# Down weight sums kept in HBM, activation sums on VectorE, and a buffer of its own for the token halves' difference, in the second feed-forward part of a Hymba layer

## The chip, the cores and the metric

The kernel is one program on one core of a Trainium2 chip. Its engines run side by side and meet at semaphores: TensorE (PE in the profile), VectorE (DVE), ScalarE (ACT), GpSimd (POOL) and SyncE (SP), which issues the transfers. The metric is the time of one execution in microseconds (us), the median of the runs.

## The reference

One layer of a Hymba decoder on 1024 tokens of 1024 features in float32: a half-step feed-forward part, a mixer (dilated attention and a Mamba-2 scan), and a second feed-forward part. The change lies in the second one:

```python
def swiglu(x, w_gate, w_up, w_down):
    return (jax.nn.silu(x @ w_gate) * (x @ w_up)) @ w_down
...
h = swiglu(rmsnorm(x, ffn2_pre_norm[i]), ffn2_w_gate[i], ffn2_w_up[i], ffn2_w_down[i])
x = x + MACARON_WEIGHT * rmsnorm(h, ffn2_post_norm[i])
```

D_FF is 2816, which makes 22 tiles of 128 hidden features, or 11 groups of two.

## The kernel before

Every float32 operand of a matmul is split in two parts that TensorE takes: hi is a rounded copy (a cast on ACT), lo is the operand less hi (a subtraction on DVE). A product is then three matmuls, hi by hi, lo by hi and hi by lo.

The second feed-forward part (f2) runs in four stages.

1. **The turn** (about 1610 to 1642 us). The first two hidden tiles are computed plainly, in rounds 0 to 3 of PE (gate_up matmuls, lines L560 to L562), while the layer's x is still being finished. Beside it DVE and ACT form the token operands that the later stage needs: s1, s2, s4 and `x_difference`, the difference of the first and the second half of the tokens (`difference`, L948 to L950, into the buffer d3, which shares its place with what rounds 0 to 2 read), times a gain, split in norm_hi and norm_lo. A planner (`turn_plan`) with a cost, the steps it depends on and a rank for each step writes the order of every engine. Lines L991 to L1013 prepare the first tile's gate and up operands.
2. **The rounds** (1642 to 2025 us). The other 20 tiles, in ten pairs i = 1 to 10 with s = 0 and 1. A tile is a block product in seven products instead of eight, with sums of gate and up weights (t_raw) and of tokens (s): product 1 to 7 of 12 matmuls each. `ffn_sp` loads each next tile, first its gate block, then two up blocks (L387, L390: g_next, v_next), each as soon as its buffer is read out, and stores the activations of the tile before to `act_scratch` in HBM (L425).
3. **Down** (2025 to 2265 us). The down projection is again seven products, m = 0 to 6, of 11 k-groups of 12 matmuls (L1517 to L1519, `down_three`). The tables DOWN_W and DOWN_B say which blocks of weights and activations product m takes: five of the seven weight operands and five of the seven activation operands are sums or differences of two blocks. For a weight sum SP loads two blocks of 256 KB (L1442) and POOL adds them (L1476, `down_w_sum`, 55 times); activation sums are on DVE for m = 1, 2, 3 and on POOL for m = 5, 6 (L1482, `down_b_sum`). Each k-group has its own slot, which product m+1 may fill when product m has used it (`down_slot`). hi parts: L1490 and L1504 on ACT. lo parts: L1508 and L1513 on DVE. `end_plan` orders all of it. `down_start_sp` starts it.
4. **The last norm.** Squares of the finished sums are added up on DVE (`square_sums`, L1758), added over features by matmuls with ones (columns, L1665), and the reciprocal root is spread over the rows by another (L1683), first for the first half of tokens, within the down products.

## Time and profile before

| what | value |
|---|---|
| median of 3 runs | 2276.1 us (2273.67 to 2276.16) |
| profiled execution, own time | 2276.56 us |
| its span in the trace | 2274.8 us |
| PE busy | 2209.6 us, 97% |
| DVE busy | 1741.1 us, 77% |
| ACT busy | 965.1 us, 42% |
| POOL busy | 350.4 us, 15% |

The span is what the trace covers; 1.8 us of the execution's time lie around it. A row of a timeline gives start, duration, engine, line and operation, tiles read and written, and in brackets how long the engine was idle ahead of it and what ended that. Times of matmuls are pipelined: 0.39 us each, but one starts every 0.227 us.

### The profile page before, as it was taken

Reading aid. Unit: us, or ns where it says so; the run is one execution under the profiler, and the core shown is the slowest. Engines: PE = TensorE matmul, PEld = TensorE weight load, DVE = VectorE, ACT = ScalarE, POOL = GpSimd, SP = SyncE. Lnnn points to the kernel's source line nnn. Section 1 sums busy time; section 2 is a strip of 40 time slices with the busy share of each in tenths; the row PEclk is TensorE's granted clock in tenths of the full one; section 3 lists DMA queues with packets and bytes.
Section 4 is the critical chain, followed back from the end, with each engine's and each line's share of the span. In section 5 each row is a group of like instructions: output and inputs, shape, how many; then the busy total and the mean of one; then the engine's idle time right before and its main releaser. Section 6 shows DMA issues by size and latency. Waiting matters only on the chain.

```text
span 2274.8 us, 29629 instructions
## 1 busy us (share of the span) xinstructions
PE 2209.6 (97%) x10304; PEld 1809.2 (80%) x10304; DVE 1741.1 (77%) x2550; ACT 965.1 (42%) x1725; POOL 350.4 (15%) x290
## 2 busy tenths in 40 slices
PE   9999999999999999999999999999899999989989
PEld 7888888888877877778788777788788888868867
DVE  8877777777759777786666676878877777789997
ACT  6322222222334576787531674224422323335443
POOL 0000000000000344444100225100000000033572
PEclk9999999999999999999999999999999999999999
DMA  4111111111323001001121234132122222285734
GB/s 161 54 53 43 54 55 55 55 40 47 117 98 125 20 10 38 29 18 57 59 82 47 75 119 174 60 100 105 53 87 83 83 83 83 83 312 201 231 116 148
DMA packets 78179, 199.83 MB, mean 88 GB/s; under 512 B 8448, under 2 KB 10496, under 8 KB 76288
## 3 DMA queue, kind: packets, MB, share of 16 engines
q1 hardware_dynamic: 78080, 198.56, 26.0%
q8 instruction: 57, 0.93, 0.2%
q14 instruction: 42, 0.34, 0.0%
HBM read 165.69 MB, written 32.83 MB: 87 GB/s over the span
## 4 chain that ended last, share of the span: by engine, by line
PE 84%; DVE 7%; ACT 3%; issue 3%; POOL 2%; DMA 1%; SPq 0%; DVEq 0%; ACTq 0%; POOLq 0%
PE psum L473 11%; PE psum L474 11%; PE psum L475 11%; PE psum L641 4%; PE psum L643 4%; PE psum L642 4%; PE psum L2437 3%; PE psum L2439 3%; PE psum L2438 3%; PE psum L1517 3%; PE psum L1519 3%; PE psum L1518 3%; PE psum L2583 2%; PE psum L2980 1%; PE psum L2594 1%
## 5 line engine op out<-in xcount | busy, mean ns | idle before, releaser
L1476 POOL TENSOR_TENSOR down_w_raw<-down_w_raw,down_w_two 128x512 f32<-128x512 f32 x55 | 88.0, 1611 | 665.0 <-DMA down_w_two<-in_d 664.9
L770 ACT CAST t_hi<-t_raw 128x512 fp32r<-128x512 f32 x152 | 93.6, 621 | 204.4 <-DVE t_raw L991 151.3
L1190 DVE TENSOR_TENSOR acc<-psum,acc 128x512 f32<-128x512 f32 x144 | 98.9, 691 | 80.5 <-PE psum L643 79.1
L792 ACT ACTIVATE sum<-sum 128x512 f32<-128x512 f32 x76 | 48.1, 633 | 231.7 <-DVE sum L1130 139.7
L1517 PE MATMUL psum<-down_b_hi,down_w_hi 128*128 128x512 f32 x308 | 123.0, 400 | 8.9 <-DVE down_w_lo L1508 8.9
L2437 PE MATMUL psum<-norm_hi,tile_hi 128*128 128x512 f32 x320 | 129.1, 403 | 1.9 <-DVE z_scaled L2845 1.9
L2754 DVE TENSOR_TENSOR probs_t_lo<-psum,probs_t_hi 128x512 fp32r<-128x512 f32 x144 | 97.1, 685 | 39.8 <-ACT probs_t_hi L2671 38.9
L473 PE MATMUL psum<-norm_hi,plain_hi 128*128 128x512 f32 x304 | 119.2, 392 | 7.5 <-DVE up_lo L1013 7.5
L2439 PE MATMUL psum<-norm_hi,tile_lo 128*128 128x512 f32 x320 | 125.0, 391 | 0.0
L2438 PE MATMUL psum<-norm_lo,tile_hi 128*128 128x512 f32 x320 | 124.8, 390 | 0.0
L766 ACT CAST plain_hi<-up_raw 128x512 fp32r<-128x512 f32 x76 | 47.1, 619 | 180.7 <-DMA up_raw<-in_gu 177.9
L2532 POOL TENSOR_TENSOR q_k_next<-first_q_k,cos 128x512 f32<-128x512 f32 x6 | 8.0, 1353 | 748.9 <-DVE first_q_k L2499 748.9
L1518 PE MATMUL psum<-down_b_lo,down_w_hi 128*128 128x512 f32 x308 | 121.8, 396 | 0.0
L1519 PE MATMUL psum<-down_b_hi,down_w_lo 128*128 128x512 f32 x308 | 121.8, 395 | 0.0
L475 PE MATMUL psum<-norm_hi,up_lo 128*128 128x512 f32 x304 | 119.0, 391 | 0.0
L474 PE MATMUL psum<-norm_lo,plain_hi 128*128 128x512 f32 x304 | 119.0, 391 | 0.0
L473 PE MATMUL psum<-norm_hi,t_hi 128*128 128x512 f32 x304 | 118.3, 389 | 0.0
L475 PE MATMUL psum<-norm_hi,t_lo 128*128 128x512 f32 x304 | 118.3, 389 | 0.0
L473 PE MATMUL psum<-s_hi,t_hi 128*128 128x512 f32 x304 | 118.3, 389 | 0.0
L474 PE MATMUL psum<-s_lo,t_hi 128*128 128x512 f32 x304 | 118.3, 389 | 0.0
L475 PE MATMUL psum<-s_hi,t_lo 128*128 128x512 f32 x304 | 118.3, 389 | 0.0
L474 PE MATMUL psum<-norm_lo,t_hi 128*128 128x512 f32 x304 | 118.3, 389 | 0.0
(456 smaller groups left out, 6477.9 us busy)
## 6 DMA issues: line engine op xcount, KB each, us to landing
down_w_raw<-in_d SPq DMA_DIRECT2D x77, 256.0 KB, 2.9
gate_raw<-in_gu SPq DMA_DIRECT2D x38, 512.0 KB, 4.3
up_raw<-in_gu SPq DMA_DIRECT2D x76, 256.0 KB, 3.9
raw_tile<-in_w_att SPq DMA_DIRECT2D x28, 512.0 KB, 3.6
down_w_two<-in_d SPq DMA_DIRECT2D x55, 256.0 KB, 4.4
act_scratch<-act_stage SPq DMA_DIRECT2D x21, 512.0 KB, 5.2
tile_lo_raw<-in_d SPq DMA_DIRECT2D x20, 512.0 KB, 4.2
x_scratch<-acc SPq DMA_DIRECT2D x32, 256.0 KB, 2.0
```

The source lines that it names most:

```text
L473: pe.matmul(o, w_hi[:, k, :], a_hi(k), start=(k == 0 and not more), stop=False, skip_group_check=more)
L474: pe.matmul(o, w_hi[:, k, :], a_lo(k), start=False, stop=False, skip_group_check=more)
L475: mm = pe.matmul(o, w_lo[:, k, :], a_hi(k), start=False, stop=(k == KH - 1), skip_group_check=more)
L770: act.copy(to, of).then_inc(sem(p + "_t_hi"), 1)
L1190: v.tensor_tensor(x, banks(4 + d % 4), x, ALU.add).then_inc(sem(p + "_acc"), 1)
L1517: pe.matmul(o, dw_hi[k][:, d, :], db_hi[k][:], start=(k == 0), stop=False)
L1518: pe.matmul(o, dw_hi[k][:, d, :], db_lo[k][:], start=False, stop=False)
L1519: return pe.matmul(o, dw_lo[k][:, d, :], db_hi[k][:], start=False, stop=(k == FG - 1))
L2437: pe.matmul(banks(bank), wh[:, w % 2, k, :], nh[:, k, x], start=(k == 0), stop=False)
L2438: pe.matmul(banks(bank), wh[:, w % 2, k, :], nl[:, k, x], start=False, stop=False)
L2439: mm = pe.matmul(banks(bank), wl[:, w % 2, k, :], nh[:, k, x], start=False, stop=(k == KT - 1))
L2754: v.tensor_tensor(ptl[:, n % 2].rearrange("p a d -> p (a d)"), banks(4 + n % 2), pth[:, n % 2].rearrange("p a d -> p (a d)").bitcast(F32), ...
```

## The change

1. *Weight sums.* POOL forms the five sums or differences of the down weights once for each k-group, during the rounds. For each of the 11 groups SP loads the two row blocks whole (two transfers of 512 KB, `w_sum_in`) at the end of a tile's loads, POOL does four operations (`w_sum_pool`: one of 128x1024 and three of 128x512), and SP stores the five sums (1.31 MB, `w_sum_out`) to a new HBM tensor `down_w_sums` in the next tile. Of the tiles n = 0 to 18 the loads stand in n = 0, 1, 3, 4, 6, 7, 9, 10, 12, 13 and 15. In the down stage every operand of weights is then one load of 256 KB, 77 in place of 132, and POOL has nothing to do there. SP's loop over the rounds is written out.
2. *Activation sums.* All 55 are on DVE.
3. *Difference.* `x_difference_turn` has its own buffer in f2. The step no longer waits for round 2, and the first t_raw sums no longer wait for the low parts of the difference. The ranks of t_hi, t_sum and t_lo in the turn are changed.

```diff
-DOWN_W = (((1, 0), (1, 1), ALU.add), ((0, 0), (1, 1), ALU.add), ((1, 1),), ((0, 1), (1, 1), ALU.subtract),
-          ((0, 0), (0, 1), ALU.add), ((0, 0),), ((1, 0), (0, 0), ALU.subtract))
+DOWN_W = {2: (1, 1), 5: (0, 0)}
+W_SUM = {4: 0, 0: 1, 1: 2, 3: 3, 6: 4}
-POOL_B = (5, 6)
...
+        d3_turn = at("x_difference_turn", 164, [P, KH, HALF])
+        wsum = nc.dram_tensor("down_w_sums", (FG, P, 5, 4, P), F32).ap()
...
             if p == "f2":
...
-                with sp.Fori(2, LAST_PAIR) as i:
-                    g_next(i, 0)
-                    v_next(i, 0, 0)
-                    store(i - 1, 1)
-                    v_next(i, 0, 1)
...
+                for n in range(2 * LAST_PAIR - 1):
+                    i, s = 1 + n // 2, n % 2
+                    g_next(i, s)
+                    v_next(i, s, 0)
+                    if n:
+                        store(1 + (n - 1) // 2, (n - 1) % 2)
...
+                    v_next(i, s, 1)
...
+                    for k in range(FG):
+                        if 3 * k // 2 == n:
+                            w_sum_in(sp, k)
+                        if 3 * k // 2 + 1 == n:
+                            w_sum_out(sp, k)
...
             def difference():
-                wait(v, p + "_gu_mm", 2 if t == "t0" else 3)
-                v.tensor_tensor(d3[:], acc[:, 0:KH, half(0)], acc[:, 0:KH, half(1)], ALU.subtract).then_inc(sem(p + "_s_dve"), 1)
+                if t == "t0":
+                    wait(v, p + "_gu_mm", 2)
+                else:
+                    v.wait_ge(sem("half_x"), past_half("t2", 1, KT) + KT)
+                v.tensor_tensor((d3 if t == "t0" else d3_turn)[:], ...)
...
             def operand_sum(n):
-                if n == 0:
-                    wait(v, p + "_s_dve", 17)
...
+        def w_sum_in(sp, k):
+            wait(sp, "dn_ws_sum", 4 * (k - 1))
+            for n in range(2):
+                sp.dma_start(ws_in[k % 2][:, n], a["d2"][FG * n + k]).then_inc(sem(f"dn_ws_in{k % 2}"), 16)
+
+        def w_sum_pool(g, k):
+            (left, right), to = (ws_in[k % 2][:, n] for n in range(2)), ws_out[k % 2]
+            wait(g, f"dn_ws_in{k % 2}", 32 * (k // 2 + 1))
+            wait(g, f"dn_ws_out{k % 2}", 16 * (k // 2))
+            g.tensor_tensor(to[:, 0:2].rearrange("p a o c -> p (a o) c"), left, right, ALU.add).then_inc(sem("dn_ws_sum"), 1)
+            g.tensor_tensor(to[:, 2], left[:, 0:4], right[:, 4:8], ALU.add).then_inc(sem("dn_ws_sum"), 1)
+            g.tensor_tensor(to[:, 3], right[:, 0:4], right[:, 4:8], ALU.subtract).then_inc(sem("dn_ws_sum"), 1)
+            g.tensor_tensor(to[:, 4], left[:, 4:8], left[:, 0:4], ALU.subtract).then_inc(sem("dn_ws_sum"), 1)
+
+        def w_sum_out(sp, k):
+            wait(sp, "dn_ws_sum", 4 * k + 4)
+            sp.dma_start(wsum[k], ws_out[k % 2][:]).then_inc(sem(f"dn_ws_out{k % 2}"), 16)
...
-            for n, (out, rows) in enumerate(DOWN_W[m][:2]):
-                to = dw_two[k] if n else dw_raw[k]
-                sp.dma_start(to[:], a["d2"][FG * rows + k][:, 4 * out:4 * out + 4]).then_inc(sem(f"dn_w_in{k}"), 16)
+            if m in W_SUM:
+                of = wsum[k][:, W_SUM[m]]
+            else:
+                out, rows = DOWN_W[m]
+                of = a["d2"][FG * rows + k][:, 4 * out:4 * out + 4]
+            sp.dma_start(dw_raw[k][:], of).then_inc(sem(f"dn_w_in{k}"), 16)
...
-                     ("ACT", "t_hi"): 7, ("DVE", "sums"): 6, ("DVE", "t_sum"): 6, ("DVE", "t_lo"): 7}
+                     ("ACT", "t_hi"): 1, ("DVE", "sums"): 6, ("DVE", "t_sum"): 1, ("DVE", "t_lo"): 0}
```

The planners then write another order. On DVE in the turn, before, from the difference's low parts (norm_lo) to the first tile's up_lo; the two gate_scaled and up_scaled near the middle belong to round 3, s1, s2 and s4 are token operands of the rounds:

```order
L954 SCALAR_TENSOR_TENSOR norm_lo_50<-x_difference_80,cols_106,norm_hi_49 128x512 x4
L977 TENSOR_TENSOR s2_lo_85<-s2_raw_86,s2_hi_84 128x2048
L981 TENSOR_TENSOR s1_lo_82<-s1_raw_83,s1_hi_81 128x2048
L2087 TENSOR_TENSOR gate_scaled_95<-psum,rstd_rows_99 128x512
L2092 TENSOR_TENSOR up_scaled_97<-psum,rstd_rows_99 128x512
L991 TENSOR_TENSOR t_raw_77<-gate_raw_71 128x512
L2096 TENSOR_TENSOR act_stage_next_186<-gate_silu_96,up_scaled_97 128x512
L985 TENSOR_TENSOR s4_lo_89<-s4_raw_90,s4_hi_a_87 128x1024
L985 TENSOR_TENSOR s4_lo_89<-s4_raw_90,s4_hi_b_88 128x1024
L997 TENSOR_TENSOR t_raw_77<-t_raw_77,up_raw_73 128x512
L1002 TENSOR_TENSOR t_raw_77<-t_raw_77,gate_raw_71 128x512
L1013 TENSOR_TENSOR up_lo_72<-up_raw_73,plain_hi_74 128x512
```

And after, from behind the difference's low parts:

```order
L995 TENSOR_TENSOR t_raw_77<-gate_raw_71 128x512
L981 TENSOR_TENSOR s2_lo_85<-s2_raw_86,s2_hi_84 128x2048
L1001 TENSOR_TENSOR t_raw_77<-t_raw_77,up_raw_73 128x512
L985 TENSOR_TENSOR s1_lo_82<-s1_raw_83,s1_hi_81 128x2048
L1006 TENSOR_TENSOR t_raw_77<-t_raw_77,gate_raw_71 128x512
L2091 TENSOR_TENSOR gate_scaled_95<-psum,rstd_rows_99 128x512
L1017 TENSOR_TENSOR up_lo_72<-up_raw_73,plain_hi_74 128x512
L1022 TENSOR_TENSOR t_lo_76<-t_raw_77,t3_hi_75 128x512
L2096 TENSOR_TENSOR up_scaled_97<-psum,rstd_rows_99 128x512
```

The low parts of s1 and s2 still stand ahead of round 3's gate, and the three sums t_raw now with them; those of s4 stand behind all of this, and up_lo stands right behind the gate. On ACT at the start of the down stage, before (w_hi and b_hi are the hi parts of a k-group's weights and activations, act_first_rows the stored activations):

```order
L792 ACTIVATE sum_2_92<-sum_2_92 128x512
L1504 CAST down_b_hi_3_239<-act_first_rows_187 128x512
L1504 CAST down_b_hi_4_240<-act_first_rows_187 128x512
L1504 CAST down_b_hi_5_241<-act_first_rows_187 128x512
L1504 CAST down_b_hi_6_242<-act_first_rows_187 128x512
L1504 CAST down_b_hi_7_243<-act_first_rows_187 128x512
L1504 CAST down_b_hi_8_244<-act_first_rows_187 128x512
L1504 CAST down_b_hi_9_245<-act_first_rows_187 128x512
L1504 CAST down_b_hi_10_246<-act_first_rows_187 128x512
L1490 CAST down_w_hi_3_195<-down_w_raw_3_228 128x512
L1490 CAST down_w_hi_4_196<-down_w_raw_4_229 128x512
L1504 CAST down_b_hi_0_236<-down_b_raw_0_258 128x512
```

After:

```order
L791 ACTIVATE sum_2_92<-sum_2_92 128x512
L1499 CAST down_w_hi_3_200<-down_w_raw_3_222 128x512
L1499 CAST down_w_hi_4_201<-down_w_raw_4_223 128x512
L1499 CAST down_w_hi_5_202<-down_w_raw_5_224 128x512
L1499 CAST down_w_hi_6_203<-down_w_raw_6_225 128x512
L1499 CAST down_w_hi_7_204<-down_w_raw_7_226 128x512
L1499 CAST down_w_hi_8_205<-down_w_raw_8_227 128x512
L1499 CAST down_w_hi_9_206<-down_w_raw_9_228 128x512
L1499 CAST down_w_hi_10_207<-down_w_raw_10_229 128x512
L1513 CAST down_b_hi_3_233<-act_first_rows_187 128x512
L1513 CAST down_b_hi_4_234<-act_first_rows_187 128x512
```

All of w_hi 3 to 10 now stands ahead of b_hi 3. On PE the two matmuls of the last norm's first half (with ones) stand, before, within product 5, the columns between its k-groups 6 and 7 and the rows between 7 and 8:

```order
L1518 MATMUL psum<-down_b_lo_6_253,down_w_hi_6_198 128x512
L1519 MATMUL psum<-down_b_hi_6_242,down_w_lo_6_220 128x512
L1665 MATMUL psum<-ones_104,square_sums_98 128x1 x4
L1517 MATMUL psum<-down_b_hi_7_243,down_w_hi_7_199 128x512
L1518 MATMUL psum<-down_b_lo_7_254,down_w_hi_7_199 128x512
L1519 MATMUL psum<-down_b_hi_7_243,down_w_lo_7_221 128x512
L1517 MATMUL psum<-down_b_hi_7_243,down_w_hi_7_199 128x512
```

After, both stand between k-group 10 of product 5 and k-group 0 of product 6:

```order
L1527 MATMUL psum<-down_b_lo_10_251,down_w_hi_10_207 128x512
L1528 MATMUL psum<-down_b_hi_10_240,down_w_lo_10_218 128x512
L1669 MATMUL psum<-ones_104,square_sums_98 128x1 x4
L1687 MATMUL psum<-square_sums_98,ones_104 128x512
L1526 MATMUL psum<-down_b_hi_0_230,down_w_hi_0_197 128x512
L1527 MATMUL psum<-down_b_lo_0_241,down_w_hi_0_197 128x512
L1528 MATMUL psum<-down_b_hi_0_230,down_w_lo_0_208 128x512
```

What moved is only these two and what DVE does for them.

## Rows read from the trace of the kernel before

**Rows 1.** Waits of PE in the whole run: us in total, times, longest.

```profile
PE psum L1665 <- DVE square_sums L1758: 9.4, 2, 9.0
PE psum L1517 <- DVE down_w_lo L1508: 8.9, 4, 6.5
...
PE psum L473 <- DVE up_lo L1013: 7.5, 1, 7.5
```

**Rows 2.** Windows: length, busy us of PE, PEld, DVE, ACT, POOL, granted clock, DMA share, GB/s.

```profile
1796.75:1834.84 38.09, 38.09 (x170) 31.54 (x169) 28.30 (x45) 11.51 (x20) 0.00 (x0) 1.00 0.26 83
1640.00:1645.00 5.00, 2.62 (x6) 2.15 (x7) 4.97 (x9) 2.90 (x5) 0.00 (x0) 0.50 0.00 0
1382.00:1384.00 2.00, 2.00 (x7) 1.57 (x6) 0.46 (x1) 0.00 (x0) 0.00 (x0) 0.59 0.93 365
```

**Rows 3.** Timeline of DVE at two tiles: start, us, line, operation, idle before.

```profile
1795.59 0.69 DVE L1013 TENSOR_TENSOR up_lo<-up_raw,plain_hi 128x512 fp32r<-128x512 f32 x1
...
1808.65 0.69 DVE L991 TENSOR_TENSOR t_raw<-gate_raw 128x512 f32<-128x512 f32 x1 [1.93 <-DMA gate_raw<-in_gu]
...
1811.99 0.68 DVE L1128 TENSOR_TENSOR sum<-psum,sum 128x512 f32<-128x512 f32 x1
```

**Rows 4.** Timeline of PE: first matmuls of product 1 and of product 7.

```profile
1796.75 0.39 PE L473 MATMUL psum<-norm_hi,plain_hi 128*128 128x512 f32 x1
...
1813.07 0.39 PE L473 MATMUL psum<-s_hi_a,plain_hi 128*128 128x512 f32 x1
```

**Rows 5.** Timeline of POOL and DVE around the last tile of the rounds.

```profile
2024.38 8.31 POOL L1476 TENSOR_TENSOR down_w_raw<-down_w_raw,down_w_two 128x512 f32<-128x512 f32 x5 [15.45 <-DMA down_w_two<-in_d]
...
2028.06 1.78 DVE L1508 TENSOR_TENSOR down_w_lo<-down_w_raw,down_w_hi 128x512 fp32r<-128x512 f32 x1
...
2029.76 0.68 DVE L1162 TENSOR_TENSOR sum<-psum,sum 128x512 f32<-128x512 f32 x1
```

**Rows 6.** Groups by line, POOL: count, busy us, mean ns of one.

```profile
L2804 POOL TENSOR_TENSOR q_k_next<-q_raw,cos 128x512 f32<-128x512 f32 x14 | 18.1, 1290 | 35.5 <-DVE q_raw L2736 35.5
...
L3244 POOL TENSOR_TENSOR square_sums<-square_sums,gate_squares 128x1024 f32<-128x1024 f32 x6 | 15.4, 2567 | 0.1
```

**Rows 7.** Timeline of DVE: a wide subtraction beside POOL.

```profile
1391.11 2.63 DVE L3131 TENSOR_TENSOR act_lo_odd<-mixed_stream,act_hi_odd 128x1024 fp32r<-128x1024 f32 x1
```

**Rows 8.** Timeline of the turn from the plain tiles to the rounds.

```profile
1624.14 0.69 DVE L2087 TENSOR_TENSOR gate_scaled<-psum,rstd_rows 128x512 f32<-128x512 f32 x1 [2.54 <-issue]
...
1634.54 0.39 PE L562 MATMUL psum<-norm_hi,gate_up_lo 128*128 128x512 f32 x1
...
1637.94 1.23 DVE L985 TENSOR_TENSOR s_lo<-s_raw,s_hi_a 128x1024 fp32r<-128x1024 f32 x1
...
1641.55 0.68 DVE L1013 TENSOR_TENSOR up_lo<-up_raw,plain_hi 128x512 fp32r<-128x512 f32 x1
...
1642.38 0.77 PE L473 MATMUL psum<-norm_hi,plain_hi 128*128 128x512 f32 x1 [7.45 <-DVE up_lo L1013]
```

**Rows 9.** Timeline at the start of the down products.

```profile
2034.47 0.34 SPq L425 DMA_DIRECT2D act_scratch<-act_stage  x1
...
2039.48 1.14 ACT L1504 CAST down_b_hi<-act_first_rows 128x512 fp32r<-128x512 f32 x2 [4.17 <-DMA act_scratch<-act_stage]
...
2043.41 0.79 PE L1517 MATMUL psum<-down_b_hi,down_w_hi 128*128 128x512 f32 x1 [6.51 <-DVE down_w_lo L1508]
```

**Rows 10.** DMA issues: count, KB each, median us to landing.

```profile
down_w_raw<-in_d SPq DMA_DIRECT2D x77, 256.0 KB, 2.9
...
gate_up_lo_raw<-in_gu SPq DMA_DIRECT2D x5, 1024.0 KB, 5.3
```

**Rows 11.** Timeline of PE before the squares' columns in product 5.

```profile
2215.95 1.84 PE L1665 MATMUL psum<-ones,square_sums 128*128 128x1 f32 x8 [9.04 <-DVE square_sums L1758]
```

**Rows 12.** Timeline of SP: the last load of a tile.

```profile
1807.96 0.33 SPq L390 DMA_DIRECT2D up_raw<-in_gu  x1
```

**Rows 13.** Timeline of PE behind a wait in the attention output.

```profile
1380.58 0.79 PE L641 MATMUL psum<-act_hi,tile_hi_first 128*128 128x512 f32 x1 [2.57 <-DVE tile_lo_first L3111]
```

More of the change, by code:

```diff
@@ L234, in build @@
         b_rows = [at("act_first_rows", 64, [P, FG, S]), at("act_second_rows", 0, [P, FG, S])]
+        ws_in = [at(f"w_sum_in_{n}", 64 + 8 * n, [P, 2, KT, P]) for n in range(2)]
+        ws_out = [at(f"w_sum_out_{n}", 80 + 10 * n, [P, 5, 4, P]) for n in range(2)]
+        d3_turn = at("x_difference_turn", 164, [P, KH, HALF])
         dsum = at("down_sums", 112, [P, KT, S])
@@ L742, in difference_hi @@
                     wait(act, p + "_gu_mm", 3)
-                act.activation(nh[:, k, half(0)], d3[:, k, :], ACT.Copy, scale=gain(k)).then_inc(sem(p + "_s_act"), 1)
+                act.activation(nh[:, k, half(0)], (d3 if t == "t0" else d3_turn)[:, k, :], ACT.Copy, scale=gain(k)).then_inc(sem(p + "_s_act"), 1)
             def s4_copy(n):
@@ L801, in tile @@
                     wait(act, p + "_read", at_tile(i, s, 11, 8 - 11))
+                    if isinstance(i, int) and i == 1 and not s:
+                        wait(act, p + "_prod", 4)
                     act.copy(e1[:], banks(0)).then_inc(sem(p + "_s_out"), 1)
@@ L1391, in build @@
         GROUPS_OF_ROWS = ((0, 4), (4, 8), (8, FG))
-        def w_loads(m):
-            return sum(min(len(x), 2) for x in DOWN_W[:m + 1])
-        def w_sums(m, k):
-            return FG * sum(len(x) > 1 for x in DOWN_W[:m]) + k + 1
         def b_sums(m, k):
-            same = [n for n in range(m) if len(DOWN_B[n]) > 1 and (n in POOL_B) == (m in POOL_B)]
-            return FG * len(same) + k + 1
+            return FG * sum(len(x) > 1 for x in DOWN_B[:m]) + k + 1
+        def w_sum_in(sp, k):
[13 more added lines that the diff above has]
+            sp.dma_start(wsum[k], ws_out[k % 2][:]).then_inc(sem(f"dn_ws_out{k % 2}"), 16)
         def puts_to(m, d):
@@ L1415, in down_b_summed @@
         def down_b_summed(eng, m, k):
-            wait(eng, "dn_b_sum_pool" if m in POOL_B else "dn_b_sum", b_sums(m, k))
+            wait(eng, "dn_b_sum", b_sums(m, k))
         def down_slot(eng, m, k):
@@ L1454, in down_start_sp @@
             sp.wait_ge(sem("act_out"), 16 * 2 * LAST_PAIR)
+            for n in range(2):
+                wait(sp, f"dn_ws_out{n}", 16 * ((FG + 1 - n) // 2))
             down_w_in(sp, 0, 0)
             down_w_in(sp, 0, 1)
-            sp.wait_ge(sem("half_out"), 16 * past_half("t3", 0, KT))
-            wait(sp, "f2_s_dve", 21)
             for g in range(3):
@@ L1598, in end_plan @@
                         if len(DOWN_B[m]) > 1:
-                            in_pool = m in POOL_B
-                            add("POOL" if in_pool else "DVE", "b_sum", ("b_sum", m, k), 1.45 if in_pool else 0.69, free)
+                            add("DVE", "b_sum", ("b_sum", m, k), 0.69, free)
                             b = ("b_sum", m, k)
@@ L1640, in end_plan @@
             rank |= {("DVE", "add"): 1, ("ACT", "put"): 1, ("DVE", "w"): 2, ("DVE", "b"): 2, ("DVE", "b_sum"): 2, ("ACT", "w"): 2,
-                     ("ACT", "b"): 2, ("DVE", "a_sum"): 3, ("DVE", "resid"): 4, ("DVE", "scale"): 5, ("POOL", "w"): 2,
-                     ("POOL", "b_sum"): 2, ("SP", "w_in"): 1}
+                     ("ACT", "b"): 2, ("DVE", "a_sum"): 3, ("DVE", "resid"): 4, ("DVE", "scale"): 5, ("SP", "w_in"): 1}
             return plan.order(rank)
@@ L1965, in turn_plan @@
             sums += [(0.69, [("resid", "t2", 1, KH + k)]) for k in range(KH)]
-            sums += [(2.2, [("round", 2, KT - 1)])] + [(0.69, [("difference_hi", k)]) for k in range(KH)]
+            sums += [(2.2, [("resid", "t2", 1, KT - 1)])] + [(0.69, [("difference_hi", k)]) for k in range(KH)]
             sums += [(2.3, [("sum_copy", 1)]), (2.3, [("sum_copy", 0)])] + [(1.22, [("s4_copy", n)]) for n in range(2)]
@@ L1972, in turn_plan @@
             for k in range(KH):
-                add("ACT", "s", ("difference_hi", k), 0.63, ("planned_sum", 12))
+                add("ACT", "s", ("difference_hi", k), 0.63, ("planned_sum", 12), ("round", 0, KT - 1))
             for n in range(2):
@@ L1977, in turn_plan @@
             for n in range(4):
[L1978 removed]
+                add("DVE", "t_sum", ("operand_sum", n), 0.69, ("seven_in",),
                     ("operand_sum", n - 1) if n else None)
@@ L3438, in _ @@
             gate_pool(g)
-            for k in range(EARLY):
-                down_w_sum(g, 0, k)
-            for step, *e in END["POOL"]:
-                if step == "w_sum":
-                    down_w_sum(g, *e)
-                else:
-                    down_b_sum(g, *e)
+            for k in range(FG):
+                w_sum_pool(g, k)
 def shape_constants():
```

46 lines of the change are left out of this document (13 added, 33 removed).

## The prediction

> **What bounds the kernel now.** I read the page first: TensorE (PE) is busy for 97% of the span, so time is gained only where PE waits, and lost wherever another engine makes it wait. The waits of PE name three places that the change touches [rows 1]: 9.4 us on the squares of the last norm, 8.9 us on a low part of a down weight, 7.5 us on up_lo. All else stays: there is no PE wait in the rounds. In two tiles of the rounds, 38.09 us, PE has no idle time, VectorE (DVE) is busy 28.30 us, GpSimd (POOL) does nothing and the DMA share is 0.26 [rows 2]. So DVE has 9.8 us to spare in 38, but not everywhere. Two places are tight. In the first, up_lo runs from 1795.59 to 1796.28 and product 1 of the next tile, which reads it, starts at 1796.75 [rows 3, 4]: slack 0.47. In the second the sum at 1811.99 reads the banks that product 7 needs, ends at 1812.67, and product 7 starts at 1813.07 [rows 3, 4]: slack 0.40. That second one hangs on a transfer: gate_raw is loaded once its last reader is done, and t_raw waits 1.93 us for it at 1808.65 [rows 3].
>
> **What POOL and DVE do to each other.** A narrow operation (128x512, two operands) on POOL takes 1.29 us [rows 6]. The DVE subtraction down_w_lo, two operands from SBUF, takes 1.78 us while POOL adds (five additions from 2024.38 on); the DVE addition at 2029.76 with one operand in PSUM takes 0.68 in the same stretch, with POOL at work too [rows 5]; up_lo with no POOL beside it took 0.69 [rows 3]. Each meeting thus adds 1.09 us to a DVE operation on SBUF alone and nothing to one that reads PSUM. A wide addition (128x1024) on POOL takes 2.57 us [rows 6]; a wide DVE subtraction that met POOL took 2.63 against 1.23 alone, +1.40 [rows 7, 8].
> The Trainium skill has this as a rule (SBUF — State Buffer, "SBUF: two separate sides"): GpSimd and a VectorE operation with two SBUF inputs take turns at one pair of ports, and whoever has it keeps it for the whole instruction. The trace agrees (1.78 against 0.68). By that rule additions that POOL does "for free" in the rounds are not free, which is the rule against this change; without it they would lie in POOL's idle time and the rival below, 2270, would be the forecast.
>
> **The change part by part.**
> *Turn.* Before, x_difference (about 2.3 us, as a wide one) waits for round 2, though DVE idled 2.54 us just before it, up to 1624.14 [rows 8]. With its own buffer it fills that idle time. The two wide low parts (about 2.3 us each) then fall under round 3, and what stands between the last matmul of round 3, at 1634.54 with 0.39 [rows 8], and product 1 shrinks from nine operations, two of them wide, to four narrow ones (gate, up_lo, t3_lo, up; the order shows it). Before, up_lo ends at 1642.23 and product 1 starts at 1642.38 [rows 8]. After: 1634.9 (the end of that matmul) + 4x0.61 (their spacing) + 0.4 for hand-overs = 1637.75. That is **-4.6**; bounds 0 (something else holds up_scaled) and -7.5, the whole wait. About 3 us of the gap stays, and with it the half clock behind it (granted 0.50 from 1640 to 1645 [rows 2]).
> *Start of down.* Product 0 of down waits at 2043.41 for k-group 3's low weight, 6.5 us [rows 1, 9], through the last tile's store (issued 2034.47, read at 2039.48 [rows 9]: 5.0 us) and POOL's sums. Without the POOL contention DVE writes act_stage about 2029.0; issue 2029.6, complete 2034.6. ACT now casts w_hi 3 to 10 ahead of b_hi 3 (order in the part on the change), and w_hi 9's load is issued only behind that store: 2034.6 + 0.5 + 2.9 for 256 KB [rows 10] = 2038.0; then w_hi 9, w_hi 10, b_hi 3, b_lo 3 at 0.62 to 0.68 and hand-overs 0.8: 2041.4. **-2.0**, a new and longer wait in the same place. Bounds: +2 (store and load each 1 later) and -8.9 (all of it gone).
> *Middle of down.* The POOL sums of weights and of activations go (55 and 22 operations); DVE gets 22 more at 0.6 us spacing, 13.2 us, and loses 1.09 at every meeting, so it has more room than before. I cost this at nothing: PE never waits there before between those places [rows 1], with DVE slower. If that cover went, 13.2 would be the price.
> *Products 5 to 6.* Before, PE waits 9.04 us for the squares [rows 11], spends 1.84 on the columns [rows 11], by my estimate 1.1 on the rows (one matmul and its hand-over) and 2.2 extra at half clock after the wait (as much as the 5 us window at 0.50 lost behind the turn's wait [rows 2]): 14.2. After, both matmuls of that norm stand right before the first matmul of product 6, behind k-group 10 of product 5 (order in the part on the change). From the end T of product 5: weight 10 is freed, issued and landed at T+3.3 (2.9 and issue); w_hi 10, b_hi 10, two casts and squares between, b_lo 10: T+6.2 to 7.0; the last square_sums T+7.6; columns 1.0, root, reciprocal, diagonal, rows, copy 3.7 in all, T+12.3. Plus 2.2 for half clock and 0.4 of issue: 14.9 against 14.2, **+0.7**. Bounds -9.0 (the wait hidden altogether) and +5 (as the single steps could be late by a whole DVE backlog of eight adds at 0.61).
> *Rounds.* Eleven bursts of four POOL additions: one 128x1024 and three 128x512, 2.57 + 3x1.29 = 6.4 us. The loads stand behind the tile's last up load (SP at 1807.96, and a tile of 19.04 us earlier at 1788.9), 1024 KB in 5.3 us [rows 10, 12], so POOL starts at about 1794.2 in the odd case (six bursts: the tile ahead of product 1 at 1796.75) and 1813.3 in the even one (five). *Odd:* the two DVE operations ahead of and at up_lo meet the wide addition (+1.40) and a narrow one (+1.09): 2.49 - 0.47 = 2.0 late at product 1. Two further meetings put the last reader of gate_raw 2.2 late, so its load and t_raw, so the sum that product 7 waits for: 2.2 - 0.40 = 1.8 to 2.0; product 3 another 0.4. Together 4.3 a burst, x6 = 25.8. PE cannot catch up, it has no idle time to give. *Even:* up_lo and the sum are already done (the sum at 1812.67); only what is due in the next tile is late: 1.0 in three, 0.2 in two, 3.4. Sum **+29**. Bounds: 0 (all fits into 9.8 us per pair) and 11x5.6 = 62 (every meeting counts: up to 2.3 where a narrow DVE operation has to wait for a whole wide addition of 2.57, and 3x1.09 for the others).
> *Clock.* After a wait of 2.57 us at 1380.58 the grant was 0.59 from 1382 to 1384 [rows 2, 13] (about 3 us at half clock, 1.4 us lost). The stalls of 2.0 are near that. I put **+3** for the rounds; bounds 0 and 12x1.4 = 17.
> *DMA.* 22 loads of 512 KB and 11 stores of 1.31 MB, about 26 MB more in 380 us of rounds, share 0.26 before [rows 2]; down drops 55 loads. A gate load beside the burst may come later; half of the 0.4 above is that.
> Sum: 2276.56 (own time; span 2274.8 and 1.8 around it; 0.4 above the median 2276.1) - 4.6 - 2.0 + 0.7 + 29 + 3 = 2302.7, against the median **2302**.
>
> **Rivals.**
> *A, the additions hide.* POOL waits its turn in DVE's idle 9.8 us, or the meetings fall on operations without a near deadline. For: DVE is a quarter idle. Against: slack of 0.47 and 0.40 at two fixed places. It gives 2276.56 - 4.6 - 2.0 + 0.7 = 2270.7, less about 0.5 to the median: 2270, faster. It turns at 6 us in all over 11 bursts, 0.54 each: below that the change is faster, above slower.
> *B, only product 1 in the odd bursts is late.* The load of gate_raw recovers in its 1.9 us: 6x2.0 = 12 instead of 29 + 3: 2276.56 - 5.9 + 12 = 2283. Against: DVE has a queue and no gap between.
> *C, every meeting counts,* even bursts too: 5.6 x 11 = 62 in place of 32: 2276.56 - 5.9 + 62 = 2332. For: in down PE waits were made of such meetings. Against: in the even case DVE's idle time of 1.93 us lies in front.
> *D, the new waits at the start of down and before product 6 swallow the gains:* +7 at most by the upper bounds, inside the forecast's own range. That the sums come too late for down is out: the last is stored four tiles before.
>
> **How the numbers follow.** The forecast has .60 (own range 2288 to 2318), A .17, B .12, C .11. The range for 8 in 10 is 2269 to 2322: it takes in half of A, B, and leaves out most of C. About 0.2%, 4.6 us, can be told from no change. Faster: nearly all of A, .16. Within 0.2%: a bit of A and the low end of B, .06. Slower: .78.
>
> **What would show it.** In the profile after, PE waits in the rounds that were not there, on up_lo at product 1 and on the psum reader at product 7, about 12 of 2 us in every second burst; DVE's two-operand subtractions with 1.7 us or more beside POOL's additions; the wait on up_lo at the turn from 7.5 to about 3; a wait at down's k-group 3 that ends on a cast of b_hi 3 behind w_hi 9; at product 6 a wait on ones and square_sums of about 12. I am wrong if the rounds show no new PE waits (then A), or if DVE operations beside POOL keep 0.69.

## The result, and the profile after

The changed kernel takes 2312.1 us (2311.4 to 2313.3, 4 runs) against 2276.1 before: ratio 1.016, 95% interval 1.0143 to 1.0178, slower by 36 us. The forecast was 2302 with its own range of 2288 to 2318. The profiled execution took 2312.59, its span is 2310.8.

The page of the changed kernel, part 1 (busy us, share of the span, instructions) and two rows of its DMA issues (count, KB each, median us to landing):

```profile
PE 2219.3 (96%) x10304; PEld 1809.6 (78%) x10304; DVE 1743.3 (75%) x2572; ACT 961.9 (42%) x1725; POOL 316.0 (14%) x257
...
down_w_sums<-w_sum_out SPq DMA_DIRECT2D x11, 1280.0 KB, 9.0
...
w_sum_in<-in_d SPq DMA_DIRECT2D x22, 512.0 KB, 7.5
```

PE has as many matmuls as before, 10304, DVE is busy for 2 us more and POOL for 34 less; no engine has become the limit. PE loses the 36 us in waiting and in running slower behind its waits. Where, the waits of PE in the changed kernel tell (us in total, times, longest; they answer to [rows 1]):

```profile
PE psum L472 <- DVE sum L1130: 18.5, 6, 5.0
PE psum L1526 <- DVE down_b_lo L1522: 9.5, 1, 9.5
PE psum L1669 <- DVE square_sums L1762: 8.4, 2, 8.0
...
PE psum L472 <- DVE t_lo L1031: 4.6, 3, 1.5
...
PE psum L472 <- ACT first_product L803: 3.4, 4, 1.9
...
PE psum L472 <- DVE up_scaled L2096: 2.6, 1, 2.6
...
PE psum L472 <- DVE up_lo L1036: 2.0, 2, 1.1
```

L472 is the first matmul of a group in the rounds. It waits 17 times there, 29.3 us in all (two more lines of the view, of 0.5 and 0.3 us, are left out above). In the kernel before it never waits there; [rows 2] has two of its tiles. The wait at the turn is down from 7.5 to 2.6 us. The starts of stages in the two profiles give the sum:

| stage | before | after | difference |
|---|---|---|---|
| start to product 1 of the first tile | 1642.38 | 1636.82 | -5.6 |
| rounds (to the first matmul of down) | 384.12 | 423.35 | +39.2 |
| down and the end | 248.3 | 250.6 | +2.3 |
| span | 2274.8 | 2310.8 | +36.0 |

Two of these rows need care. The first is one profile against one: in the profiles of the twelve kernels of the next section, all with the own buffer and the same work up to there, product 1 starts between 1632.3 and 1641.3 us, so only the shorter wait, 4.8 us, is sure. The second counts from a start that was poor: in the kernel before, the granted clock was 0.50 from 1640 to 1645 [rows 2], which cost its first tile 1.9 us, and its first matmul of down waited 1.1 us. The changed kernel has neither. This is its grant behind the turn's wait (columns as in [rows 2]):

```profile
1636.80:1641.80 5.00, 4.98 (x22) 4.13 (x23) 4.81 (x8) 2.33 (x5) 0.00 (x0) 1.00 0.00 0
```

Rounds with neither take 381.2 us (the kernel with the own buffer alone, below), so the additions make them 42 us longer, not 39.

One of the long waits is worth reading from its cause to its end. First the stretch around a burst (DVE and POOL of the changed kernel's timeline):

```profile
1807.49 2.90 POOL L1407 TENSOR_TENSOR w_sum_out<-w_sum_in 128x1024 f32<-128x1024 f32 x1 [16.12 <-DMA w_sum_in<-in_d]
1810.35 1.75 POOL L1408 TENSOR_TENSOR w_sum_out<-w_sum_in 128x512 f32<-128x512 f32 x1
```

```profile
1808.05 0.68 DVE L1164 TENSOR_TENSOR sum<-psum,sum 128x512 f32<-128x512 f32 x1
1808.76 2.17 DVE L1166 TENSOR_TENSOR sum<-sum,rstd_rows 128x512 f32<-128x512 f32 x1
1810.86 1.78 DVE L1036 TENSOR_TENSOR up_lo<-up_raw,plain_hi 128x512 fp32r<-128x512 f32 x1
1812.57 1.77 DVE L1040 TENSOR_TENSOR t_lo<-t_raw,t_hi 128x512 fp32r<-128x512 f32 x1
1814.26 1.77 DVE L1174 TENSOR_TENSOR act_stage<-up,sum 128x512 f32<-128x512 f32 x1
1815.96 0.68 DVE L1044 TENSOR_TENSOR gate_lo<-gate_raw,plain_hi 128x512 fp32r<-128x512 f32 x1
```

The same operation in the same tile of the kernel before, whose product 1 starts at 1796.75 [rows 4]; in the changed kernel it starts at 1804.64:

```profile
1803.29 0.69 DVE L1040 TENSOR_TENSOR gate_lo<-gate_raw,plain_hi 128x512 fp32r<-128x512 f32 x1
```

The operation with an operand in PSUM keeps its 0.68 us beside POOL; each of the four that follow takes 1.77 to 2.17 while the four additions run (0.69 alone [rows 3]). POOL pays as well: its narrow additions take 1.74 instead of 1.29 [rows 6]. The four DVE operations together take 4.7 us more than alone. gate_lo, the last reader of gate_raw, so ends 12.0 us behind product 1, where it ended 7.2 behind it before. Then SP, DVE and PE:

```profile
1816.66 0.33 SPq L390 DMA_DIRECT2D gate_raw<-in_gu  x1
1817.03 0.43 SPq L393 DMA_DIRECT2D up_raw<-in_gu  x1
...
1821.34 0.69 DVE L995 TENSOR_TENSOR t_raw<-gate_raw 128x512 f32<-128x512 f32 x1 [3.38 <-PE psum L474]
...
1822.75 0.69 DVE L1001 TENSOR_TENSOR t_raw<-t_raw,up_raw 128x512 f32<-128x512 f32 x1 [0.72 <-DMA up_raw<-in_gu]
...
1825.29 0.68 DVE L1130 TENSOR_TENSOR sum<-psum,sum 128x512 f32<-128x512 f32 x1
```

```profile
1826.03 0.80 PE L472 MATMUL psum<-s_hi_a,plain_hi 128*128 128x512 f32 x1 [4.81 <-DVE sum L1130]
```

The gate load goes out when gate_lo is done and lands 4.6 us later, at 1821.3, and t_raw starts. (Its bracket names PE, but the matmuls that it waits for were long done; in the kernel before the same wait is put down to the load [rows 3], which went out 4.5 us ahead.) The sum that empties the banks for product 7 is queued behind t_raw on DVE: PE waits 4.81 us. The windows of the same kernel (columns as in [rows 2]) show the burst, with DVE full for 8.46 of 8.5 us, and the lower clock behind the long wait, granted 0.59 (a grant of 0.50 is the lower of its two levels, 1.2 GHz, called half clock here; this stretch is mostly at it):

```profile
1807.50:1816.00 8.50, 8.50 (x39) 6.88 (x38) 8.46 (x8) 1.63 (x3) 7.98 (x4) 1.00 0.00 0
1826.00:1831.00 5.00, 4.97 (x13) 3.93 (x14) 4.73 (x8) 2.36 (x4) 0.00 (x0) 0.59 0.09 37
```

Not every burst of four additions costs the same. Counted from the starts of product 1 in the timelines (tiles n = 0 to 19, 19.04 us each when PE never waits):

| burst of k-group | POOL begins | waits of PE | tile is longer by |
|---|---|---|---|
| 1, 5, 9 | 2.9 to 4.2 us into tiles 2, 8, 14 | one of 4.8 to 5.0 at product 7 | 7.3, 7.1, 7.9 us |
| 2, 6, 10 | 0.8 to 1.0 us ahead of tiles 4, 10, 16 | 1.5, 0.5 and 1.1 to 1.4, at products 3, 4 and 7 | 4.5, 4.7, 4.6 us |
| 3, 4, 7, 8 | 0 to 1.3 us into tiles 5, 7, 11, 13 | at most one, of 0.5 to 1.9, at product 4 or the next product 1 | 1.4, 2.2, 0.9, 1.2 us |
| 0 | 1.1 us ahead of tile 1 | none | 0 |

The first two rows are the prediction's six odd bursts: 36 of the 42 us.

### The profile page after: what moved, and what is told of

Same layout as the page of the kernel before. It is cut to its first block, busy times and chain, and to the rows that moved or that the text cites. A ratio compares the mean times of both kernels' runs of the same rounds, so it can differ in the third digit from the quotient of the medians.

```text
span 2310.8 us, 29395 instructions
## 1 busy us (share of the span) xinstructions
PE 2219.3 (96%) x10304; PEld 1809.6 (78%) x10304; DVE 1743.3 (75%) x2572; ACT 961.9 (42%) x1725; POOL 316.0 (14%) x257
## 4 chain that ended last, share of the span: by engine, by line
PE 76%; DVE 12%; issue 4%; ACT 3%; DMA 3%; POOL 1%; DVEq 0%; SPq 0%; ACTq 0%; POOLq 0%
PE psum L472 8%; PE psum L473 7%; PE psum L474 7%; PE psum L640 4%; PE psum L641 4%; PE psum L642 4%; PE psum L1526 3%; PE psum L1528 3%; PE psum L1527 3%; PE psum L2441 3%; PE psum L2442 3%; PE psum L2443 3%; PE psum L2587 2%; DMA up_raw<-in_gu 1%; PE psum L2984 1%
## 5 line engine op out<-in xcount | busy, mean ns | idle before, releaser
L472 PE MATMUL psum<-norm_hi,plain_hi 128*128 128x512 f32 x304 | 119.5, 393 | 8.7 <-ACT first_product L803 3.4
L472 PE MATMUL psum<-s_hi,t_hi 128*128 128x512 f32 x304 | 118.6, 390 | 4.6 <-DVE t_lo L1031 4.6
L472 PE MATMUL psum<-norm_hi,t_hi 128*128 128x512 f32 x304 | 118.7, 391 | 0.6 <-DVE sum L1111 0.3
L640 PE MATMUL psum<-act_hi,tile_hi 128*128 128x512 f32 x288 | 112.0, 389 | 0.0
L641 PE MATMUL psum<-act_lo,tile_hi 128*128 128x512 f32 x288 | 112.0, 389 | 0.0
```

Of the source, the lines that this page charges most:

```text
L472: pe.matmul(o, w_hi[:, k, :], a_hi(k), start=(k == 0 and not more), stop=False, skip_group_check=more)
L640: pe.matmul(o, w_h[:, s, d, :], a_h[:, s, x], start=(s == 0), stop=False)
L641: pe.matmul(o, w_h[:, s, d, :], a_l[:, s, x], start=False, stop=False)
```

## The experiments

Times are medians, each with its ratio to the kernel before, which was run beside it (its median there is 2274.4 to 2276.9). Stage times are from the one profile of each kernel. Two theories stood against each other for the rounds. M: the meetings of POOL and DVE cost the time. T: the 26 MB of new traffic make the gate and up loads late.

**The third edit alone, on the kernel before.**

```diff
-                wait(v, p + "_gu_mm", 2 if t == "t0" else 3)
-                v.tensor_tensor(d3[:], acc...
...
+                    v.wait_ge(sem("half_x"), past_half("t2", 1, KT) + KT)
+                v.tensor_tensor((d3 if t == "t0" else d3_turn)[:], acc...
...
```

> The kernel before with only the third edit: the difference in its own buffer, the turn's waits and ranks changed, all sums as before. My theory: PE's 7.5 us wait on up_lo at the turn becomes 2.6 as in the changed kernel and nothing else moves, since the down stage and the rounds are untouched: 5 us less, 2271. Rival (the gain is given back later, because the tile behind starts with the same loads in flight): 2276, no change.

Measured: 2270.2 us, ratio 0.9972 (0.9961 to 0.9984), 5.7 us less. As expected; the wait is 2.6 us, and the rounds behind it take 381.2 us in place of 384.1. A part is given back: the wait for the squares in product 5 rose from 9.0 to 11.2 us.

**The sums' transfers without the additions.** From the third k-group on:

```diff
-            g.tensor_tensor(to[:, 2], left[:, 0:4], right[:, 4:8], ALU.add)
...
+            c = P if k < 2 else 4
...
+            g.tensor_tensor(to[:, 2, :, 0:c], left[:, 0:4, 0:c], right[:, 4:8, 0:c], ALU.add)
...
```

> The changed kernel with GpSimd's additions cut from 128 to 4 columns of each block from the third k-group on (the down weights' sums are left unformed there), every transfer, wait and semaphore kept. Theory M (meetings of GpSimd and VectorE at SBUF cost the time): of the 17 waits of PE in the rounds only those of the first two groups stay, one of 5.0 and its half clock; the rounds give back about 32 of 39 us: 2280. Theory T (the 26 MB more of traffic make the gate and up loads late): the 4.8 to 5.0 us waits at product 7 stay, 2300 to 2312.

Measured: 2279.4 us, ratio 1.0011 (1.0000 to 1.0021). M expected 2280. One wait of PE is left in the rounds, behind the second burst, which was kept:

```profile
PE psum L472 <- DVE sum L1130: 3.5, 1, 3.5
```

The rounds take 387.6 us, nearly all of the excess in tile 2; from tile 4 on every tile takes 19.0 to 19.1 us. So the traffic by itself costs PE nothing in the rounds.

**The additions without the stores.**

```diff
-            sp.dma_start(wsum[k], ws_out[k % 2][:])
+            sp.dma_start(wsum[k][:, 0, 0:1], ws_out[k % 2][:, 0, 0:1])
...
```

> The changed kernel with the 11 stores of 1.28 MB cut to one block of 128x128 each, and the down weights loaded as single blocks straight from the input (sums not used). GpSimd's additions are all there, but their operands land earlier. Theory M: the additions still meet VectorE, the sum of PE's waits in the rounds stays within 20 to 40 us, only its places change: 2295 to 2312. Theory T (the store ahead of the loads is what hurts): the 5 us waits go and nothing comes, 2285 or less.

Measured: 2304.8 us, ratio 1.0129 (1.0106 to 1.0151). The answer of the waits of PE:

```profile
PE psum L472 <- ACT first_product L803: 13.9, 9, 1.9
...
PE psum L472 <- DVE t_lo L1031: 6.6, 7, 1.4
PE psum L472 <- DVE sum L1130: 6.3, 5, 1.3
```

With one of 0.9 on up_lo that is 27.7 us of waiting instead of 29.3, in 22 waits of at most 1.9. So the meetings stay, as M says, but the three waits of 5 us are gone. The reason isn't that gate_lo comes in time. In tile 8, whose product 1 starts at 1805.60 here, it is as late as in the changed kernel:

```profile
1805.83 2.40 POOL L1407 TENSOR_TENSOR w_sum_out<-w_sum_in 128x1024 f32<-128x1024 f32 x1 [15.11 <-DMA w_sum_in<-in_d]
...
1816.90 0.68 DVE L1044 TENSOR_TENSOR gate_lo<-gate_raw,plain_hi 128x512 fp32r<-128x512 f32 x1
...
1822.34 0.69 DVE L995 TENSOR_TENSOR t_raw<-gate_raw 128x512 f32<-128x512 f32 x1 [3.42 <-DMA gate_raw<-in_gu]
...
1826.60 0.50 PE L472 MATMUL psum<-s_hi_a,plain_hi 128*128 128x512 f32 x1 [1.25 <-DVE sum L1130]
```

gate_lo ends 12.0 us and t_raw starts 16.7 us behind product 1, in both kernels. What the store changes is when the burst begins: the loads of groups 1, 3, 5, 7 and 9 go out right behind a store, and POOL begins 9.3 to 10.6 us behind the first of them, but 6.9 to 7.7 when the store is cut. So in tile 8 the burst begins 0.2 us into the tile instead of 2.9 and also holds what products 3 and 4 need: PE waits 1.1, 1.6 and 1.25 us there and at product 7 where it waited 4.8 once, and the clock stays full. The same tile, from product 1 to product 1, in the changed kernel and in this one (columns as in [rows 2]):

```profile
1804.64:1830.78 26.14, 21.33 (x86) 16.99 (x85) 21.47 (x28) 6.26 (x11) 8.00 (x4) 0.87 0.41 142
```

```profile
1805.60:1829.47 23.87, 19.96 (x85) 15.53 (x84) 19.62 (x25) 5.65 (x10) 7.47 (x4) 1.00 0.22 69
```

The three tiles with the long waits are 7.6 us shorter in all, others are 3.0 longer: the rounds take 418.8 us, 4.6 less than in the changed kernel. The rest of the 7.4 us between the medians lies outside the rounds.

**No weight sums at all.**

```diff
-                        if 3 * k // 2 == n:
-                            w_sum_in(sp, k)
-                        if 3 * k // 2 + 1 == n:
-                            w_sum_out(sp, k)
...
-            for k in range(FG):
-                w_sum_pool(g, k)
```

> The changed kernel without anything of the weight sums in the rounds: no loads, no additions, no stores; down weights are loaded as single blocks (the sums are left out). It is the floor of this design, what the other two edits and a down stage without GpSimd are worth. Both theories: rounds back at 384 us, so 39 less: 2273; the down stage should be 1 or 2 us slower than before, as in the changed kernel. If it is well below 2271, the traffic of the down stage matters too.

Measured: 2268.3 us, ratio 0.9968 (0.9956 to 0.9979), 4.7 less than expected. The rounds take 381.3 us: I had put them at the kernel before's 384, which has the half clock and the wait of its poor start in it. Down to the end takes 249.2, 0.9 more than before, as expected. The rest of the change is worth 7.7 us, and forming the sums in the rounds costs 36.0 + 7.7 = 43.7.

**The second edit, with the own buffer.** `POOL_B = ()` beside the first experiment's edit; weight sums stay on POOL in the down stage.

> The kernel before with the difference in its own buffer and all activation sums on VectorE; weight sums as before on POOL in the down stage. Beside the kernel with the own buffer alone (2270) it tells what the second edit does. Theory: 22 operations more on VectorE, but 22 meetings of 1.09 us less, so about even, and the 11 us wait for the squares in product 5 gets shorter by a few us, as fewer of POOL's operations stand there: 2266 to 2270. Rival (VectorE is the full engine there, 13 us more on it show): 2273 or more.

Measured: 2281.8 us, ratio 1.0022 (1.0013 to 1.0030): 11.7 us slower than the own buffer alone (+5.9 against -5.7). I had expected no loss; the rival holds, and by more than it said. The loss lies at the squares: from k-group 3 of the first down product to the last matmul of down it takes 230.0 us, 219.7 with the own buffer alone. The wait for the squares in product 5 is now at product 6 and 17.9 us:

```profile
2231.84 1.84 PE L1669 MATMUL psum<-ones,square_sums 128*128 128x1 f32 x8 [17.94 <-DVE square_sums L1762]
2234.97 2.08 PE L1687 MATMUL psum<-square_sums,ones 128*128 128x512 f32 x2 [1.29 <-DVE square_sums L1682]
```

So "cover" for the 22 operations was only there because POOL leaves the down stage in the changed kernel: that is worth 13.6 us, from +5.9 here to -7.7 without any weight sums. That step takes away POOL's 55 additions and 55 loads together; no run parts the two. Put in a row, the kernels part the 36 us as -5.7 (own buffer), +11.7 (activation sums), -13.6 (no weight sums in down) and +43.7 (sums in the rounds). Each part is the difference of two neighbours in the row, so the parts add up to the whole whatever they are; in another order of the edits they could be other numbers.

**The same additions in VectorE's idle places.** Five additions of 128x512 for a k-group, each with a wait on DVE's own progress. A tile of the second kind is one with s = 1, n odd in the code; one of the first kind has s = 0:

```diff
+        POCKETS = [(n, name, of, at) for n in range(1, 2 * LAST_PAIR - 1)
+                   for name, of, at in ([("f2_t_lo", 7, 7)] * (1 + n % 2) + [("f2_read", 11, 2)] + [("f2_read", 11, 3)] * (n % 2))]
...
+                n, name, of, at = POCKETS[5 * k + j]
+                wait(g, name, at_tile(1 + n // 2, n % 2, of, at))
+                g.tensor_tensor(to[:, j], one, two, op).then_inc(sem("dn_ws_sum"), 1)
...
```

> The changed kernel with the same sums and the same transfers, but each k-group's work as five additions of 128x512, and each addition started by VectorE's own progress at a place where VectorE then idles (behind the last low part of a tile and behind the first reads of the products' banks: 1.1 to 2.4 us idle in the profile before), three to four in a tile of the second kind and two in the first. Theory: it isn't the amount of POOL work that costs but that a burst of four meets VectorE just ahead of product 1, 3 and 7; here PE's waits in the rounds fall from 29 us to under 8: 2272 to 2282. Rival (each addition costs wherever it stands, at 1.09 us for each of 55, two thirds of it on PE): 2300 or more.

Measured: 2275.9 us, ratio 0.9998 (0.9989 to 1.0008). PE has no wait in the rounds. POOL's group of additions, and one place in the timeline of DVE:

```profile
L1416 POOL TENSOR_TENSOR w_sum_out<-w_sum_in 128x512 f32<-128x512 f32 x55 | 70.6, 1290 | 493.6 <-DVE gate_lo L1044 458.5 <-DVE sum L1111 25.8 <-DVE up L1125 9.4
```

```profile
1852.88 0.68 DVE L1044 TENSOR_TENSOR gate_lo<-gate_raw,plain_hi 128x512 fp32r<-128x512 f32 x1
1855.89 0.69 DVE L1109 TENSOR_TENSOR sum<-psum,first_product 128x512 f32<-128x512 f32 x1 [2.33 <-PE psum L474]
```

All 55 additions take 1.29 us each, as alone; the narrow ones of the changed kernel take 1.74. So the rounds cost nothing, and the kernel is no faster than the one before: there is a new wait of 6.2 us at the first matmul of down. The last store goes out at 1997.6, and SP's first load for down, which waits for all stores, at 2002.1.

**The same single additions in full places.** The waits are on PE's products 5 to 7 and the next product 1:

```diff
+                   for at in ((5, 6, 7, 8) if n % 2 else (6, 7)) for name, of in (("f2_seven", 7),)]
...
```

> The same five single additions a group, in the same tiles as in the kernel with VectorE's idle places (2275.9), without the k-group order, but each started when PE ends product 5, 6, 7 or the next tile's product 1, where VectorE has no idle time. Theory (the place decides, not the number or the burst): PE waits in the rounds come back, at 0.4 to 0.9 us an addition: 2298 to 2325. Rival (single additions are harmless anywhere, bursts are not): 2276 to 2282.

Measured: 2319.2 us, ratio 1.0194 (1.0175 to 1.0213). In the profiles the rounds take 420.0 us to the last product's end against 381.1 with the idle places; this is what the places cost. The wait at the first matmul of down is 13.5 against 6.2, and that belongs to the last store, which goes out 15 us ahead of the end of the rounds here and 21 ahead there. In the rounds PE waits again:

```profile
PE psum L472 <- DVE sum L1130: 13.7, 8, 3.9
...
PE psum L472 <- DVE up_lo L1017: 10.1, 9, 2.1
```

Same count, same size, no burst: the place decides.

**The bursts whole, but placed.** Each starts behind gate_lo, nine in tiles of the second kind:

```diff
+        W_TILE = (1, 3, 5, 6, 7, 9, 11, 12, 13, 15, 17)
...
+            wait(g, "f2_t_lo", at_tile(1 + W_TILE[k] // 2, W_TILE[k] % 2, 7, 7))
...
```

> The changed kernel with its bursts of one wide and three narrow additions whole, but each started behind the last low part of a tile (gate_lo), nine of them in tiles of the second kind, where VectorE idles 5.7 us in the next 8, two in the first kind. Theory: most of a burst of 6.4 us then lies in idle time, and 0 to 1.5 us of PE is lost in each, 2 to 3 in the two others: 2276 to 2288. Rival (a burst hurts wherever it starts, because it holds the first reads of the banks that follow): 2300 or more.

Measured: 2271.6 us, ratio 0.9975 (0.9965 to 0.9986), below the expected range. Two waits of 0.6 us are left in the rounds, in the two tiles of the first kind. It is no faster than the own buffer alone (2270.2): with their places well chosen the sums in the rounds cost next to nothing, and the rest of the change brings nothing yet.

**The start of down.** In four kernels ACT's and DVE's first steps are put in the order of the k-groups:

```diff
         END = end_plan()
+        for engine, steps in (("ACT", ("w_hi", "b_hi")), ("DVE", ("w_lo", "b_lo"))):
+            first = [e for e in END[engine] if e[0] in steps and e[1] == 0]
+            END[engine] = sorted(first, key=lambda e: (e[2], steps.index(e[0]))) + [e for e in END[engine] if e not in first]
```

On the kernel before with the own buffer:

> The kernel before with the difference in its own buffer, and with ACT's and DVE's first down steps in the order of the k-groups: w_hi 3, b_hi 3, w_hi 4, b_hi 4 and so on, where before all b_hi 3 to 10 stood ahead of w_hi 3. Theory: group 3's 6.5 us wait at the start of down is one for the last tile's store only because b_hi 9, which reads it, is queued ahead of w_hi 3; with it gone 6 or 7 us of 2270 go: 2264. Rival: the wait moves to group 9 or to DVE, since DVE is full there: 2268 to 2270.

Measured: 2269.8 us, ratio 0.9967 (0.9954 to 0.9980), the same as without (2270.2). The rival holds: the 6.5 us wait is gone, but seven waits on down_w_lo add up to 7.2 and the one for the squares is 14.0 instead of 11.2.

On the kernel with the idle places:

> The additions in VectorE's idle places and the order by k-groups at the start of down together, on the changed kernel. Here the 9.5 us wait at group 3 ends on b_lo 3 behind w_hi 9 and 10, whose load is issued behind the store. Theory: 8 us less than the kernel with the additions in the idle places alone, 2264 to 2274, and no wait over 3 us left at the start of down. Rival: the 9.5 us turn up again at group 9, since that load still waits for a store of 7.7 us: only 2 or 3 less.

Measured: 2267.3 us, ratio 0.9956 (0.9943 to 0.9968), 8.6 less than without. The wait at group 3 is gone (in the kernel without this edit it was 5.0 us, not the 9.5 of the changed kernel); the one at the first matmul of down stays and is 7.1 us, so "no wait over 3 us" did not come true. The same edit is worth 8.6 where POOL is out of the down stage and nothing where it is in it.

With a later wait for the last two stores:

```diff
-                wait(sp, f"dn_ws_out{n}", 16 * ((FG + 1 - n) // 2))
+                wait(sp, f"dn_ws_out{n}", 16 * ((FG - 1 - n) // 2))
...
+            for n in range(2):
+                wait(sp, f"dn_ws_out{n}", 16 * ((FG + 1 - n) // 2))
             store(LAST_PAIR, 1)
```

> The kernel with the additions in VectorE's idle places and the k-group order, and one thing more: at the start of down SP waits for the stores of the sums of groups 9 and 10 only ahead of the loads of those groups, where it waited for all 11 ahead of the first load. Theory: the 7.1 us wait of PE at the first product of down is this store, issued late in the last tile but one; with it gone, 7 us and its half clock go: 2258 to 2261. Rival: the transfers at the start of down then meet the store and the rows of activations and turn up as a wait at group 3 to 10: 2264 to 2267.

Measured: 2264.0 us, ratio 0.9945 (0.9932 to 0.9959). That is the rival's number but not its place: 3.1 us are left at the first matmul of down, and there is no wait at groups 3 to 10.

And on the bursts placed:

> The bursts placed behind gate_lo (2271.6 by themselves), and the order by k-groups at the start of down. There 9.9 us of waiting at group 3 were left and no store of sums is late. Theory: these 9.9 us and their half clock go, and nothing takes their place: 2260 to 2263, the fastest of all. Rival: about 3 us come back at the first groups of down as in the last kernel, then 2264.

Measured: 2260.1 us (2258.7 to 2261.5), ratio 0.9930 (0.9914 to 0.9946), as expected: 0.7% or some 15 us faster than the kernel before (14.3 by the two medians, 2260.1 and 2274.4, 16 by the ratio), and some 10 less than the placed bursts alone. There is no wait left at the start of down. Beside the own buffer and the same order of steps without the sums in HBM, 2269.8, the weight sums and activation sums together are worth 8 to 10 us here. Its waits of PE:

```profile
PE psum L1672 <- DVE square_sums L1765: 8.4, 2, 8.1
...
PE psum L472 <- DVE up_scaled L2102: 2.6, 1, 2.6
```

## Why the prediction was right, and where its terms were off

*The mechanism* was the one named: additions on POOL hold up DVE operations on SBUF alone, at places with 0.4 to 0.5 us of slack. The transfers alone, at 2279.4, and the same additions in idle and in full places, at 2275.9 and 2319.2, show it. Rival A (it all hides) is what happens only when the places are chosen; B (2283) and C (2332) are out by size. The forecast of 2302 is 10 us short: against the terms of its sum the rounds came out 7.2 higher, down 3.6 higher and the turn 1.0 lower.

*The rounds* were sized at 29 + 3. They are 39.2 longer than before and 42 longer than rounds with the same start. That 29.3 us of waits were found where 29 were forecast is in good part luck. The six odd bursts did carry nearly all, 36 us (forecast 25.8 and the clock), the others 6 (forecast 3.4). But the places were only half right: product 7 was forecast at 1.8 to 2.0 in each odd burst, 11 to 12 in all, and waits 18.5; product 1 was forecast at 2.0 in each, 12 in all, and waits once, 0.5 us; product 3 was forecast at 2.4 in all and waits 4.6; product 4 was not in the forecast and waits 5.4 (first_product and up_lo). Two things in the step were wrong. The landing was taken from other loads, 5.3 us [rows 10]; here the 512 KB loads took 7.5 by the median, and in the stretch shown, right behind a store, POOL began 10.8 us behind the tile's last up load (1796.67 to 1807.49). So the bursts met the tile 1.5 to 6.7 us later than I had them. And the chain through gate_raw was sized by two meetings (2.2 us late); in the stretch shown four met it, 4.7 us.

*The clock*: the 29.3 us of waits make 42 of lost time. About 6 are matmuls at half clock behind the three long waits, 2 each, where 3 were put for the whole. The rest is that every wait is counted from the modelled end of a matmul, 0.16 after the next could have started (0.39 less 0.227), and that delays shorter than this show as no wait at all: some 6 to 7 us. At the turn I had the half clock stay behind a wait of about 3 us; the wait stayed at 2.6, the half clock is gone in the changed kernel, and that is 1.9 us which no term of the forecast had.

*The turn* was sized -4.6 and is -5.6 in these two profiles, of which 4.8 are the wait. *The start of down* was sized -2.0 and is 0: the last tile's product 7 ends at 2060.2 and group 3 starts at 2078.1, 17.9 us, as before (18.0). What was wrong there is the store of the last tile, taken at 5.0 us: it was issued at 2064.48 and took 7.7 (4.9 before), and the load of group 9, which waits for it, went out at 2072.26. The order of ACT, w_hi 9 ahead of b_hi 3, did make it a 9.5 us wait as said. *Products 5 to 6* were right in kind, with 8.0 + 1.3 + 0.8 us of waiting for "about 12", and in time within a microsecond, as far as it can be told apart: from group 3 to the end it is 1.3 longer than before, for +0.7, and as long as with the own buffer alone (219.7 us of down). *The middle of down at nothing* came out right in the sum and wrong as an argument for the edit itself: 22 more operations on DVE cost 11.7 us while POOL works beside it. I had counted 13.2 as the price if the cover went, and the cover is POOL's leaving.

The three waits of 5 us come only with groups 1, 5 and 9, and the timelines show why. These are the bursts whose loads go out right behind a store in a tile with n odd, so that POOL begins 2.9 to 4.2 us into the next tile: behind the DVE operations that products 3 and 4 need, but ahead of gate_lo. All the lateness then comes out at product 7. Groups 2, 6 and 10 make gate_lo just as late (it ends 11.7 us behind product 1), but PE has by then waited 2 us at products 3 and 4. What stays open is which part of the 13.6 us in down is POOL's additions and which its 55 loads.

## What to carry to other kernels

An idle engine that shares something with a full one isn't idle capacity: price its work in the full engine's time, and at the places with the least slack, not by its mean idle share. If it must run there, start each piece by the full engine's own progress, where the profile shows that engine waiting: the same 11 bursts made the rounds 42 us longer (423.4 against 381.3) when their landing started them, and 2 to 3 (383.1 and 384.5 in its two kernels) when gate_lo did. And try an edit's parts alone: here one was worth -5.7, and one +11.7 that another's -13.6 paid for. And look at how the stage that a change frees begins: with the bursts placed, the whole change was no faster than its buffer alone (2271.6 and 2270.2), until ACT's and DVE's first steps in down were reordered too (2260.1).
